# Twelve chunks instead of thirteen: 128, 96 and 64 slots for ranked experts, on one Trainium2 core

## The reference, cut to what matters

```python
expert_id = g_idx * EXPERTS_PER_GROUP + top_i            # 512 tokens x 2
comb = jnp.sum(jax.nn.one_hot(expert_id, N_EXPERTS) * weights[..., None], axis=1)
def step(acc, xs):
    wg, wu, wd, cw = xs                                   # 1024x256, 1024x256, 256x1024
    y = (jax.nn.silu(t @ wg) * (t @ wu)) @ wd
    return acc + y.astype(jnp.float32) * cw[:, None], None
```

## Time and profile before

| | us |
|---|---|
| median of 3 runs (lowest, highest) | 1961.71 (1959.69, 1963.35) |
| the profiled execution | 1962.96 |
| its span, first to last instruction | 1961.3 |
| TensorE busy / VectorE / ScalarE / GpSimd | 1910.7 / 748.5 / 550.6 / 727.3 |
| mean granted TensorE clock | 0.993 of full speed |

### The profile page before, as it was taken

The page is one execution under the profiler, slowest core; times in us unless marked ns, Lnnn a source line. Parts: engine busy times, 40 slices in busy tenths (PEclk is TensorE's granted clock), DMA queues, the critical chain, the costliest instruction groups (busy, mean ns, idle before and its releaser), DMA issues.

```text
span 1961.3 us, 24433 instructions
## 1 busy us (share of the span) xinstructions
PE 1910.7 (97%) x9028; PEld 1030.4 (53%) x9028; DVE 748.5 (38%) x1628; ACT 550.6 (28%) x1197; POOL 727.3 (37%) x1053
## 2 busy tenths in 40 slices
PE   8999999999999999999999999999999999998998
PEld 6645556656457454565665455654444444444444
DVE  1243443433112243443445563843532401325333
ACT  3243432214321344422124322742211221013110
POOL 0767676765667667676610012100110100001101
PEclk9999999999999999999999999999999999998999
DMA  7332443244344353343384312041799722126996
GB/s 294 120 113 96 137 137 127 82 148 141 132 168 141 105 198 113 129 138 115 137 326 171 129 38 86 2 191 53 299 409 374 260 74 84 70 123 234 395 410 242
DMA packets 72149, 330.63 MB, mean 169 GB/s; under 512 B 8617, under 2 KB 11111, under 8 KB 57447
## 3 DMA queue, kind: packets, MB, share of 16 engines
q1 hardware_dynamic: 41688, 216.93, 29.2%
q0 software_dynamic: 26896, 99.63, 14.6%
q10 hardware_dynamic: 3456, 12.58, 1.6%
HBM read 289.27 MB, written 39.85 MB: 168 GB/s over the span
## 4 chain that ended last, share of the span: by engine, by line
PE 88%; DMA 5%; DVE 3%; issue 2%; ACT 1%; DVEq 1%; SPq 0%; POOL 0%; ACTq 0%; POOLq 0%
PE psA L464 25%; PE psA L1799 10%; PE psA L456 9%; PE psA L1934 7%; PE psA L1836 6%; PE psA L627 6%; PE psSO L1952 4%; PE psT L443 3%; PE psA L505 3%; PE psSO L534 3%; DMA pool_mem<-in_w_dn 2%; PE psSO L544 2%; DVE pool_mem L2861 1%; PE psSO L565 1%; PE psSO L600 1%
## 5 line engine op out<-in xcount | busy, mean ns | idle before, releaser
L464 PE MATMUL psA<-gB,pool_mem 128*128 128x512 f32 x1024 | 455.3, 597 | 0.0
L395 POOL TENSOR_TENSOR pool_mem<-pool_mem,cs 128x256 f32<-128x256 f32 x448 | 269.7, 635 | 129.1 <-DMA pool_mem<-in_mod_w 128.4
L464 PEld LDWEIGHTS psA<-gB,pool_mem 128*128 128x128 f32 x1024 | 189.5, 190 | 224.2 <-issue 224.2
L399 POOL TENSOR_TENSOR pool_mem<-pool_mem 128x256 f32<-128x256 f32 x336 | 248.2, 767 | 33.4 <-issue 25.4
L1799 PE MATMUL psA<-pool_mem 128*128 128x512 f32 (+1 forms) x528 | 210.6, 558 | 6.0 <-DVE pool_mem L1570 3.4
L456 PE MATMUL psA<-pool_mem,gB 128*128 128x256 f32 (+2 forms) x768 | 190.7, 404 | 2.6 <-ACT gB L797 1.6
L1748 POOL DMA_INDIRECT pool_mem<-xs_scratch,idx x32 | 30.6, 955 | 387.4 <-DVE idx L2551 360.7
L456 PEld LDWEIGHTS psA<-pool_mem,gB 128*128 128x128 f32 x768 | 144.5, 191 | 45.4 <-issue 7.5
L1934 PE MATMUL psA<-pool_mem 128*128 128x512 f32 (+1 forms) x448 | 158.1, 609 | 5.5 <-DMA pool_mem<-in_w_dn 5.5
L1799 PEld LDWEIGHTS psA<-pool_mem 128*128 128x128 f32 x528 | 100.4, 192 | 109.7 <-issue 99.8
L1836 PE MATMUL psA<-pool_mem 128*128 128x512 f32 x256 | 113.9, 595 | 0.8 <-issue 0.8
(11 more groups left out here) (339 smaller groups left out, 2381.2 us busy)
## 6 DMA issues: line engine op xcount, KB each, us to landing
pool_mem<-in_w_gu SPq DMA_DIRECT2D x32, 2048.0 KB, 19.2
pool_mem<-in_mod_w POOLq DMA_DIRECT2D x56, 1024.0 KB, 7.9
pool_mem<-in_w_dn SPq DMA_DIRECT2D x32, 1024.0 KB, 17.0
pool_mem<-in_w_qk SPq DMA_DIRECT2D x24, 1024.0 KB, 5.2
ys_scratch<-pool_mem ACTq DMA_DIRECT2D x24, 512.0 KB, 10.5
ys_scratch<-pool_mem POOLq DMA_DIRECT2D x1, 11264.0 KB, 42.1
pool_mem<-in_odd_w_in SPq DMA_DIRECT2D x5, 2048.0 KB, 9.6
pool_mem<-in_w_out SPq DMA_DIRECT2D x4, 2048.0 KB, 9.0
```

The costliest lines, as they stand in the source:

```text
L395: nc.gpsimd.tensor_tensor(wm[:, b, k], wm[:, b, k], c_all[:, k].to_broadcast([P, MCH]), ALU.mult)
L399: nc.gpsimd.tensor_tensor(wm[:, b, k], wm[:, b, k], wm[:, b, n + k], ALU.add)
L464: m = nc.tensor.matmul(psA[:, n % 2, :], w(i), src[:, k, :], start=(i == 0), stop=(i == len(ks) - 1))
```

## The change

There are now three sizes: ranks 0 to 4 have 128 slots, ranks 5 to 10 have 96, ranks 11 to 15 have 64. The order is 12 runs: F F F X X F X X F X X P, where each X in `ORDER` gives two runs, each with a 96-slot expert in columns 0 to 95 and one half (32 slots) of a 64-slot expert in 96 to 127; the 64-slot expert is shared by both. `STRIPS` splits the 96 columns into 64 and 32, so that the products of such a run are three per k step: 64, 32 and 32 columns of the array. The ranking is by token count now, with ties by number, the experts 0 to 2 first (`STATIC = 3`). `later` holds the row numbers of slots 32 to 63 in partitions 0 to 31 for the second half of a split expert. `places()` is in three parts: `planned()` under run 1's gate and up, `overflow_planned()` and `places()` under run 2's, `weights()` and `last_weights()` under run 3's. SP waits for the plan and chunk 1's gather before use 3.

```diff
-FULL, HALF = 10, 64
-STATIC = 4
-ORDER = "FFFFFPFFPFFPF"
...
+STATIC = 3
+SIZES = (P,) * 5 + (96,) * 6 + (64,) * 5
+ORDER = "FFFXFXFXP"
+def plan_runs():
+    fulls, wide, split, halves = [list(r) for r in (range(5), range(5, 11), range(11, 14), range(14, 16))]
...
+        elif kind == "P":
+            runs.append(((halves.pop(0), 0, 0, 64), (halves.pop(0), 0, 64, P)))
+        else:
+            r = split.pop(0)
+            for first in (0, 32):
+                runs.append(((wide.pop(0), 0, 0, 96), (r, first, 96, P)))
...
+STRIPS = [[(r, a, b) for r, _, lo, hi in parts for a, b in (((lo, lo + 64), (lo + 64, hi)) if hi - lo == 96 else ((lo, hi),))]
+          for parts in PARTS]
...
-                sp.wait_ge(xg_loaded[0], GATHERED[0] * l + 32)
+                sp.wait_ge(plan_ready, 2 * l + 1)
+                sp.wait_ge(xg_loaded[1], GATHERED[1] * l + 16)
                 for u in range(EARLY, EXPERTS):
-                    if USES[u] == STATIC:
-                        sp.wait_ge(plan_ready, 2 * l + 1)
...
-                            nc.gpsimd.tensor_copy(idx1[:, j:j + 1], idx[:, ds(e, 1)]).then_inc(idx_moved, 1)
+                            nc.gpsimd.tensor_copy(idx1[:, j:j + 1], (later if first else idx)[:, ds(e, 1)]).then_inc(idx_moved, 1)
...
                     for k in range(KD):
-                        for r, lo, hi in PARTS[c]:
+                        for r, lo, hi in STRIPS[c]:
                             m = nc.tensor.matmul(psA[lo:hi, b, :], xgT[:, b, k, lo:hi], gu_w[USES.index(r) % EXP_BUFS][:, k, :],
                                                  start=(k == 0), stop=(k == KD - 1))
...
                         for k in range(2):
-                            for r, lo, hi in PARTS[c]:
+                            for r, lo, hi in STRIPS[c]:
                                 m = nc.tensor.matmul(psO[lo:hi, half, :], hidT[:, b, k * P + lo:k * P + hi],
...
-                nc.vector.scalar_tensor_tensor(full, last, float(HALF), static, ALU.is_gt, ALU.max)
+                nc.vector.scalar_tensor_tensor(full, last, float(EXPERTS), prefer, ALU.mult, ALU.add)
...
                 nc.vector.tensor_copy(idx[:, 0:EXPERTS], psS[:, 0, 0:EXPERTS]).then_inc(own_ready, 1)
+                nc.vector.tensor_copy(later[0:32, :], psS[32:64, 0, 0:EXPERTS])
...
+                def planned():
+                    for found, known in ((cap, sizes), (base, bases), (jump, jumps)):
+                        nc.vector.tensor_tensor(square, each(rank, EXPERTS), along(eno, EXPERTS, EXPERTS), ALU.is_equal)
+                        dve.drain()
+                        nc.vector.tensor_tensor(square, square, along(known, EXPERTS, EXPERTS), ALU.mult)
+                        dve.drain()
+                        nc.vector.tensor_reduce(found, square, AX.X, ALU.add)
+                        dve.drain()
...
-                    nc.vector.tensor_tensor(hot, iota.rearrange("p (o n) -> p o n", o=1).to_broadcast([P, TOP * NT, P]),
...
+                    for i, hot in enumerate((comb_rows, second)):
+                        nc.vector.tensor_tensor(hot, along(iota, NT, P), each(relm[:, NT * i:NT * i + NT], P), ALU.is_equal)
+                        dve.drain()
+                        nc.vector.tensor_tensor(hot, hot, each(wts[:, i, :], P), ALU.mult)
...
                     if c == 0:
+                        planned()
+                    elif c == 1:
+                        overflow_planned()
                         places()
-                    elif c == 1:
+                    elif c == 2:
                         weights()
                         last_weights()
```

More of the change, by code:

```diff
@@ L1244 @@
 TOP = 2
-FULL, HALF = 10, 64
-PAIRED = EXPERTS - FULL
-STATIC = 4
-ORDER = "FFFFFPFFPFFPF"
[L1251 to L1260, removed]
-RUNS = len(PARTS)
-USES = [r for parts in PARTS for r, _, _ in parts]
-RUN_OF = {r: c for c, parts in enumerate(PARTS) for r, _, _ in parts}
-MOVES = EXPERTS - STATIC
+STATIC = 3
[3 more added lines that the diff above has]
+    fulls, wide, split, halves = [list(r) for r in (range(5), range(5, 11), range(11, 14), range(14, 16))]
+    runs = []
+    for kind in ORDER:
+        if kind == "F":
+            runs.append(((fulls.pop(0), 0, 0, P),))
+        elif kind == "P":
[4 more added lines that the diff above has]
+                runs.append(((wide.pop(0), 0, 0, 96), (r, first, 96, P)))
+    return runs
+PARTS = plan_runs()
+RUNS = len(PARTS)
+ROWS = [P * c for c in range(RUNS)]
+USES = list(dict.fromkeys(r for parts in PARTS for r, _, _, _ in parts))
+RUN_OF = {r: c for c, parts in enumerate(PARTS) for r, _, _, _ in parts}
+BASES = {r: ROWS[c] + lo for c, parts in enumerate(PARTS) for r, first, lo, _ in parts if first == 0}
+JUMPS = {r: ROWS[c] + lo - first - BASES[r] for c, parts in enumerate(PARTS) for r, first, lo, _ in parts if first}
+STRIPS = [[(r, a, b) for r, _, lo, hi in parts for a, b in (((lo, lo + 64), (lo + 64, hi)) if hi - lo == 96 else ((lo, hi),))]
+          for parts in PARTS]
+MOVES = sum(1 for parts in PARTS for r, _, _, _ in parts if r >= STATIC)
 LOADED = [32 * len(USES[b::EXP_BUFS]) for b in range(EXP_BUFS)]
@@ L1269 @@
 LAST_END = ROWS[-1] + P
-OVER = 9
+OVER = 10
 YS_ROWS = P * (RUNS + OVER)
@@ L1362, in second_block @@
     eno, first4, earlier, ranked, static = table(EXPERTS), table(EG), table(EG, EG), table(TOP, EG), table(EXPERTS)
+    prefer, sizes, bases, jumps = (table(EXPERTS) for _ in range(4))
     jthr, mno, othr = table(NT), table(OVER), table(OVER + 1)
@@ L1414, in second_block @@
     idx = sb("idx", [P, EXPERTS + OVER], I32)
+    later = sb("later", [P, EXPERTS], I32)
     idx1 = sb("idx1", [P, 4], I32)
@@ L1737, in gather @@
                     b = c % 2
-                    for i, (r, lo, hi) in enumerate(PARTS[c]):
+                    for i, (r, first, lo, hi) in enumerate(PARTS[c]):
                         if r < STATIC:
@@ L1922, in weights @@
                 def weights(c):
-                    for r, _, _ in PARTS[c]:
+                    for r, _, _, _ in PARTS[c]:
                         u = USES.index(r)
@@ L2435, in add_output @@
                     nc.vector.memset(rtw_flat[:, DEPTH * KD * 20:], 0.0)
+                    nc.vector.memset(later[:], 0)
                     dve.drain()
@@ L2566, in experts @@
                 route(l)
-                def places():
+                def planned():
                     last = cnt[:, NT, :]
[L2570 to L2575, removed]
+                    square = big[:, 0:EXPERTS * EXPERTS].rearrange("p (e j) -> p e j", e=EXPERTS)
+                    for found, known in ((cap, sizes), (base, bases), (jump, jumps)):
[5 more added lines that the diff above has]
+                        dve.drain()
                     nc.vector.tensor_tensor(excl, last, cap, ALU.subtract)
-                    nc.vector.tensor_tensor(at_slot, cnt[:, 0:NT, :], along(cap, NT, EXPERTS), ALU.is_ge)
                     dve.drain()
@@ L2993, in layouts @@
         both(np.arange(16)[None]), both(np.arange(4, 0, -1)[None]), both(np.tri(4, 4, -1).reshape(1, 16)),
-        both((np.arange(2)[:, None] - 3 + np.arange(4)[None]).reshape(1, 8)), both((np.arange(16) < STATIC)[None]),
+        both((np.arange(2)[:, None] - 3 + np.arange(4)[None]).reshape(1, 8)), both(np.where(np.arange(16) < STATIC, 20000 - np.arange(16), 0)[None]),
+        both(15 - np.arange(16)[None]), both(np.array(SIZES)[None]), both(np.array([BASES[r] for r in range(16)])[None]),
+        both(np.array([JUMPS.get(r, 0) for r in range(16)])[None]),
         both(128 * np.arange(4)[None]), both(np.arange(OVER)[None]), both(OVER_AT + 128 * np.arange(OVER + 1)[None])],
```

28 lines of the change are left out of this document (17 added, 11 removed).

## The result

The changed kernel takes **2104.05 us** (median of 4 runs, 2102.72 to 2111.13) against 1961.99 (4 runs, 1959.69 to 1963.35): the ratio over all runs is 1.0735 times the time before, 95% interval 1.0719 to 1.0751 (the two medians alone give 1.0724). The profiled execution took 2105.06 us, its span is 2103.5. The forecast was 2104. It was right in the mechanism and in the size of its main term.

The account below looks back on a forecast made before the run. The prediction took TensorE as the bound (busy in 97% of the span, 88% of the chain). Runs +140.2 us over both layers, weight waits -8.4 and chunk 2's gather +10.8 made +142.6 on 1961.71: 2104 us, range 2075 to 2130.

Parts of the forecast that it names:

- The mixed run: TensorE's expert stage: six runs of 64, 32 and 32 columns per layer, each 13.8 us over a full run, +82.8.
- Run count, pairs, weight waits: Expert stage: per layer one run less -11.4 us, two paired runs fewer -1.3; weight waits and slow products gone, -8.4 altogether.
- Chunk 2's gather: Start of the expert stage: the gather lands late beside the weight loads and TensorE waits, +10.8 us for both layers.
- The layers' ends: What follows the last run's down in each layer: forecast as unchanged, 0 us in both layers.
- widths side by side: Mixed products on TensorE: strips of different widths overlap, -15 us, giving 1946 us (1935 to 1955); chance 0.10.
- waits for own strips only: Mixed products on TensorE: a width switch costs 0.09 us but waits only for its own strips, 1981 us; chance 0.04.
- a lower clock: Mixed products on TensorE: the half-filled array lowers the clock, +247 us, giving 2351 us; chance 0.03.
- overflow chunk: Expert stage: an expert beyond its slots would add a serial chunk, at least 11.4 us; chance 0.01.

Follow-up runs that it names:

- grouped: The changed kernel with each mixed product doing all k steps of the 64 strip first, then all of the 32 strips: 2077.56 us, ratio 1.0595.
- the repeat: The changed kernel run again unaltered, in another set and compared with the kernel before: 2098.01 us, ratio 1.0696.
- the first experiment: The changed kernel with the 96 columns cut into 32 + 32 + 32 instead of 64 + 32, so all strips are equal: 1965.71 us, ratio 1.0023.

## Why the forecast was right, and where it wasn't

- **The mixed run, +82.8 per layer.** Right, and shown from four sides: alternating widths 15.95 us, grouped 14.07, equal 7.07, and the same 15.95 in the kernel before. The step was forecast at 1.98 us from attention's rows; it came out at 1.99 (2.06 less the overlap of 0.07), and eight steps of 1.98 with the last recorded end make the 15.95. That a switch of width empties the array held for 128x64 against 128x32 too, where no row of before had shown it. The rule of the Trainium skill (TensorEngine Tiling, Tiling Modes, Key Properties) that a change of tiling mode drains the engine agrees. The rule that tiles in different column groups overlap (TensorE: Matmul & The Clock Gate, Part 3) agrees at one width (7.07, four strips) and not between two widths (15.95).
- **Run count, pairs, weight waits.** Right: runs 1 to the last came to +64.3 and +66.2 against 65.6 and 66.2; the waits of the earlier trace rows are gone.
- **Chunk 2's gather, +10.8.** Too large. SP's first load came at 1384.34, not 1383.2. In the repeat, where the landing is on record, chunk 1's gather took 5.2 us (1377.80 to 1383.0) and the load followed 1.1 us later. The probable reason is that SP must now read the number of use 3's expert from the plan first, as it didn't in the kernel before; the forecast had no time for that. In layer 0 of the first profile chunk 2's gather then had 1.3 us on free queues and was in time. It was late in one layer of two in each profile: for most of the +3.8 in the first, and for 1.56 us of the +4.0 in the repeat, where 2.5 us stand before it, in slower products behind chunk 0's gather (7.32 us from 1380.86 to 1388.18 against 4.80 before, granted clock 0.58 from 1380 to 1388). The forecast had 5.4 in both layers. That the step taken was the worst overlap (a gather issued with the weights, 11.2 us to land) was the error: the two race, and the forecast should have had half of it.
- **The layers' ends, forecast at nothing.** Missed. I had read the stage up to the last run only. In layer 0 the projection's 2 MB and the store of the last run but one meet more closely, and the combine's gathers wait for that store: +3.7 and +4.6. The variant that moves the load shows it (store 2.6 us instead of 7.5, wait gone), and that 2.2 us are given back elsewhere. In layer 1 the end was 5.4 us longer in the profile with ScalarE's late copy and 0.1 in the other.
- **The sum.** The two errors cancelled: the gather came out 7.0 us below the forecast (7.8 in the repeat), the ends 9.1 above (4.7). Against the repeat (2098.0) the forecast is 6 us high.
- **The rival "widths side by side", 1946.** Its condition was false. Its price was wrong as well: the first experiment makes it true and gives 1965.7. The rival had let the weight waits go or stay at 8.4 us; with shorter runs and full queues they grow to 17. The share of 1.00 stood in the prediction, and its price didn't use it.
- **The other rivals** (waits for own strips only, 1981; a lower clock, 2351) are excluded by 15.95 and by a granted clock of 1.00 in the stage. No overflow chunk ran.

What stays open: why ScalarE's copy is late in some executions. Behind the branch that skips the overflow chunks it sat idle 12.1 to 12.9 us in layer 1 in four profiles: after, equal widths, grouped widths, and four strips in the kernel before (there 11.3 in layer 0 too). In the other eight it started as soon as its operand was there, after 8.7 to 8.9 us (13.2 with 64, 32 and 32 columns in the kernel before, where the last down is longer). The changed kernel is among both. The record of packets shows two instruction packets behind the branch in both executions: one of 8 KB near 2074.5 and 2074.4, and one of 16 KB near 2082.0, 3.9 us ahead of the late copy, and near 2080.7, 1.3 us ahead of the timely one. Whether ScalarE waits for what one of them brings isn't shown. Only one execution of each set is profiled, so it isn't shown either how much of the 6 us between the two medians of the changed kernel is this copy, and how much the chip.

## What to carry to other kernels

In these float32 products strips of 64 and of 32 columns don't run beside each other on TensorE, strips of one width do; cut 96 + 32 as four strips of 32, not as 64 + 32 + 32, and if two widths must meet, put all k steps of one before those of the other. Before counting a saved run of an engine as time, ask how much of it the queues have left: where their share is already 1.00, a run less is a longer wait for weights. And a difference of 5 us between two builds isn't an effect of the edit until the unaltered kernel has run again beside it.

## What the runs showed of the hardware that I hadn't expected

- Instruction count was nearly free here: 64 instructions of 128x32 take 7.07 us where 16 of 128x128 take 7.03.
- When an indirect gather is issued just ahead of large loads, less than a microsecond decides. Issued 0.16 us (1856.37, first load 1856.53) and 0.52 us ahead (repeat, layer 0: 1383.58, 1384.10) chunk 2's gather landed after 10.9 and some 10.6 us; 1.05 us and 1.34 us ahead (1860.36, 1861.41; 1383.00, 1384.34) it was there within 7.3. The width variants agree in layer 1: 0.40 us ahead with four strips (1786.24, 1786.64) it took some 11.5 us, 0.78 us ahead with grouped widths (1846.98, 1847.76) it was there within 7.7.
- One and the same kernel, its copy on ScalarE: 12.66 us of idle time in one execution, 8.85 in the other, and 6 us between the medians of two sets of four runs, perhaps on different chips, more than the 0.2% that I had taken for the limit of what can be told.
